# Moving the activation buffers 192 bytes on and leaving out three products per feed-forward stage

## The chip, the cores and the metric

The kernel runs on one NeuronCore of a Trainium2 chip. The metric is the device time of one execution in microseconds (us), lower is better. Before the change the median of three runs is 1860.11 us, the lowest 1859.53 and the highest 1865.53.

## What is computed

Ten layers in a row act on one sequence of 256 tokens with 1024 features (T = 256, D = 1024). Each layer normalises x, scales and shifts it by a modulation vector made from a condition c, applies a mixer or a feed-forward network, and adds the gated result to x:

```python
for st, kind in enumerate(["ffn", "mamba", "ffn", "ffn", "moba", "ffn", "sb", "cffn", "dsa", "cffn"]):
    shift, scale, gate = split(silu(c) @ mod_w[st] + mod_b[st], 3)
    h = rmsnorm(x, g[st]) * (1 + scale) + shift
    y = layer[kind](h)          # ffn: (silu(h @ w_gate) * (h @ w_up)) @ w_down, D_FF = 2816
    x = x + gate * y            # times 0.5 behind an ffn of the first block
```

"mamba" is a chunked state-space scan, "moba", "sb" and "dsa" are attention layers, "cffn" is a feed-forward network with a short convolution. All weights are float32 and each is used once: 276 blocks of 1 MB.

## The kernel before, in words

Everything is kept transposed: a tile has 128 partitions of features and 256 columns of tokens. A block of weights is a tile of 128 x 2048 float32. SyncE's queue loads block after block into six slots `raw0` to `raw5`. ScalarE rounds a block to a high part `w_hi` (type float32r, a form of float32 that TensorE multiplies in one pass), VectorE subtracts it from the block and writes the low part `w_lo`; there are three slots of each. The activations are split in the same way, into `h_hi` and `h_lo` behind the normalisation, and into `a_hi` and `a_lo` behind the nonlinearity. A product is then three matmuls by the helper `three`: high with high (L1413), high weights with the low activations (L1414), low weights with the high activations (L1415). Each is 128 x 128 stationary against 128 x 256 moving, and each has a weight load of its own (PEld in the profile) that overlaps the matmul before it. The stationary operand is the weights and the moving one the activations, with one exception: in "moba" and "sb" the value blocks (`tokens=True`) load `h` as the stationary operand and stream `w`.

A feed-forward stage has eleven triples of blocks (gate, up, down), 48 matmuls a block, in a fixed program order on TensorE: gate of block column n, up of n, down of n - 1. Semaphores order the engines: `wlo` counts finished splits, `blk` counts blocks that TensorE has finished with. The first gate block of a stage goes by a form of its own (L1426, L1428 and L1433): all products that need `h_hi` first, one feature tile after another as the normalisation delivers them, then those that need `h_lo`. Behind it the helper `in_step` issues three matmuls (L1453) in which the high part of the next block is both the stationary and the moving operand, into PSUM bank 6, where nobody reads them. The six feed-forward stages (four "ffn", two "cffn") share this program.

The buffers lie in SBUF in the order in which they are made. The program allots them one after another from a fixed start, each rounded up to a multiple of 32 bytes in every partition. These lines (L212 to L228) set what the change touches:

```python
raw = [sb(f"raw{s}", [P, 2048]) for s in range(NRAW)]
w_hi = [sb(f"w_hi{s}", [P, 2048], F32R) for s in range(NW)]
w_lo = [sb(f"w_lo{s}", [P, 2048], F32R) for s in range(NW)]
x = sb("x", [P, KT, T])
folded3 = sb("folded3", [P, 3, 96])
gs = sb("gs", [P, NJOB, 8])
h_hi = sb("h_hi", [P, KT, T], F32R)
```

Behind them follow `h_lo`, `work`, the modulation buffers, parameters and constants, `ws_hi` and `ws_lo` (a few small projection weights, also used through `three`), `a_hi`, `a_lo` and the large scratch tile `mix`. From the sizes in these lines: the six weight slots all start at the same remainder of 256 bytes (8192 bytes each); `h_hi` starts 6 x 8192 + 8192 + 1152 + 320 = 58816 bytes behind `w_hi0`, which is 229 x 256 + 192. `a_hi` starts 147904 bytes behind `w_hi0`, which is 577 x 256 + 192. So h and a both lie 192 bytes behind the weights by remainder of 256, which is the same as 64 bytes before them. Every slice that a matmul takes of w, h or a is a multiple of 512 bytes on, so this distance is the same in all of them. In the value blocks, where the operands change places, the moving one lies 64 bytes behind the stationary one.

Of the kernel before, what the change touches and what calls it, by code (L numbers as in the profile page):

```python
# [27 lines left out]
P = 128  # L28
T = 256
D = 1024  # L30
KT = D // P
# [179 lines left out]
def build(nc, weights, mods, params, consts, xin, out, stages=None):  # L211
# [3 lines left out]
    with ExitStack() as ctx:  # L215
        def sb(name, shape, dt=F32):
            return ctx.enter_context(nc.sbuf_tensor(name, shape, dt))
# [5 lines left out]
        folded3 = sb("folded3", [P, 3, 96])  # L223
        folded = [folded3[:, n, :] for n in range(3)]
        gs = sb("gs", [P, NJOB, 8])
        h_hi = sb("h_hi", [P, KT, T], F32R)
        h_lo = sb("h_lo", [P, KT, T], F32R)
        work = sb("work", [P, KT * T])  # L228
# [25 lines left out]
        bank = [ctx.enter_context(nc.psum_tensor(f"bank{n}", [P, 512], F32)) for n in range(8)]  # L254
# [1147 lines left out]
        def _(eng):  # L1402
            k = Steps(eng, plan, sems)

            def begin(st, i, a, b):

                eng.wait_ge(sems["wlo"], k.block(st, i, a, b) + 1)
                s = k.block(st, 0 if a % NW == 0 else i, a, b) % NW
                return [w[s][:, :] for w in (w_hi, w_lo)]
# [35 lines left out]
                                           kk == 0, kk == KT - 1)  # L1445
                mm.then_inc(sems["blk"], 1)

            def in_step(st, b):


                hi = begin(st, 0, 0, b)[0].rearrange("p (k n) -> p k n", k=KT)
                for kk in range(3):
                    eng.matmul(bank[6][:, 0:T], hi[:, kk, 0:P], hi[:, kk, :], start=True, stop=True)  # L1453

            def gemm_out(st, i=0, a=0, b=0, ready=None, fresh=False):

                hi, lo = [w.rearrange("p (k n) -> p k n", k=2) for w in begin(st, i, a, b)]
                for kk in range(2):
                    ready(kk)
                    for m in range(KT):  # L1460
                        part = slice(m * P, (m + 1) * P)
                        mm = three(acc(m), hi[:, kk, part], lo[:, kk, part], a_hi[:, kk, :], a_lo[:, kk, :],
                                   fresh and kk == m % 2 == 0, False, True)
                mm.then_inc(sems["blk"], 1)
# [32 lines left out]
            def ffn(st):  # L1497
                kind = stages[st]
                free4, per4, free5, per5 = ("silu", 1, "mul", 1) if kind == "ffn" else ("tap2", 2, "tap2", 2)

                def gate(i, a, b, first=False):
                    if not first:
                        k.wait(free4, st, i, per4, -per4)
                    gemm(bank[4], st, i, a, b, first=first)

                def up(i, a, b, first=False):
                    if not first:
                        k.wait(free5, st, i, per5, -1)
                    gemm(bank[5], st, i, a, b)

                def down(i, a, b, fresh=False):
                    gemm_out(st, i, a, b, lambda kk: k.wait("alo", st, i, 1, -1) if kk == 0 else None, fresh)

                gate(0, 0, 0, True)
                in_step(st, 1)
                up(0, 0, 1, True)
                gate(1, 3, -1)
                up(1, 3, 0)
                down(1, 3, 1, True)
                for i in k.loop(2, NFB - 1):  # L1520
                    gate(i, 3, -1)
                    up(i, 3, 0)
                    down(i, 3, 1)
                n = NFB - 1
                gate(n, 3, -1)
                up(n, 3, 0)
                down(n, 3, 1)
                last(st, lambda: k.wait("alo", st, b=n))

            def last(st, ready):  # L1530

                hi, lo = [w.rearrange("p (k n) -> p k n", k=2) for w in begin(st, 0, 0, NBLK[stages[st]] - 1)]
                ready()
                ffn = stages[st] in ("ffn", "cffn")
                ahi, alo = (z_hi, z_lo) if ffn else (a_hi, a_lo)
                more = st + 1 < NST
                if st == 0:
                    eng.wait_ge(sems["const"], 1)
                    eng.wait_ge(sems["late"], 2)
                    eng.wait_ge(sems["go"], KT + 2)  # L1540
                    eng.matmul(bank[7][:, 96:128], con_("fold"), gfold, start=True,
                               stop=True).then_inc(sems["gmods"], 1)
                if more:
                    modulation(st + 1)
                for pair in range(4):
                    if pair == 3 and more:
                        squares(st + 1, 0)
                    for m in (2 * pair, 2 * pair + 1):
                        part = slice(m * P, (m + 1) * P)
                        for kk in range(2):  # L1550
                            mm = three(acc(m), hi[:, kk, part], lo[:, kk, part], ahi[:, kk, :], alo[:, kk, :],
                                       False, False, True)
                    if pair < 3:
                        k.inc("pair", mm)
                    else:
                        mm.then_inc(sems["blk"], 1)
                if more:
                    squares(st + 1, 1)
                    squares(st + 1, 2)
                    squares(st + 1, 3)  # L1560
# [261 lines left out]
            def sparse_front(st):  # L1822
# [28 lines left out]
                for h in range(8):  # L1851
                    if h >= 2:
# [4 lines left out]
                k.wait("rel", st, b=7)  # L1857

            programs = {"ffn": ffn, "cffn": ffn, "mamba": mamba, "moba": lambda st: heads(st, "moba"),
                        "sb": lambda st: heads(st, "sb"), "dsa": lambda st: heads(st, "dsa")}  # L1860
            eng.wait_ge(s_ones, 16)
# [115 lines left out]
```

## Time and profile before

| | before |
|---|---|
| median of 3 runs | 1860.11 us (1859.53 to 1865.53) |
| the profiled execution | 1870.03 us, its span 1868.2 us |
| TensorE busy in the span | 1773.6 us, 95% |
| VectorE, ScalarE busy | 77%, 51% |
| mean granted clock of TensorE | 0.98 |
| DMA, mean over the span | 228 GB/s |

Busy shares alone tell little here. A matmul is pipelined, its recorded duration (about 280 ns) is longer than the distance to the next one, and TensorE is "busy" in 95% of the span whether its matmuls follow each other quickly or slowly. What tells is the distance between the starts of two matmuls, or, for a stretch without waits, the length of the stretch over the number of matmuls in it.

### The profile page before, as it was taken

To read this page: it belongs to the slowest core of one execution; us is meant where nothing else is said; L and a number is where in the kernel's file an instruction comes from. 1 tells how busy PE (TensorE), PEld (TensorE's weight loads), DVE (VectorE), ACT (ScalarE), POOL (GpSimd) and SP (SyncE) were. 2 spreads that over 40 slices of the span, in tenths; PEclk is the share of its full clock that TensorE was granted. 3 is DMA by queue.
4 is the path that set the end of the run, shared out by engine and by line. 5 is a ranking of instruction groups with operands and counts; after the bars stand their busy time and mean duration, and the time that the engine had idled before them with its cause. 6 is when DMAs were issued, how large, how long until landed. Compare 5 with 4: busy or idle time off the path is not lost.

```text
span 1868.2 us, 34057 instructions
## 1 busy us (share of the span) xinstructions
PE 1773.6 (95%) x14608; PEld 1718.4 (92%) x14608; DVE 1441.2 (77%) x1714; ACT 961.6 (51%) x1257; POOL 0.2 (0%) x4
## 2 busy tenths in 40 slices
PE   5999999999999999999989999898998999999999
PEld 4999999998899999999979999898898988889999
DVE  7799888887789779986557897655799777447776
ACT  4433466666434454445564433655644555666554
POOL 0000000000000000000000000000000000000000
PEclk8999999998999999999999999999999998999999
DMA  9999734433699759983426997243395534324551
GB/s 396 418 403 364 289 113 158 158 139 133 228 373 365 293 202 379 362 330 123 181 94 240 378 367 273 112 158 113 123 344 186 202 139 171 132 97 163 191 191 46
DMA packets 68149, 426.23 MB, mean 228 GB/s; under 512 B 7488, under 2 KB 10832, under 8 KB 31824
## 3 DMA queue, kind: packets, MB, share of 16 engines
q1 hardware_dynamic: 63936, 416.22, 58.3%
q10 hardware_dynamic: 4112, 8.62, 1.4%
q8 instruction: 68, 1.11, 0.2%
q14 instruction: 33, 0.27, 0.0%
HBM read 423.74 MB, written 3.17 MB: 229 GB/s over the span
## 4 chain that ended last, share of the span: by engine, by line
PE 85%; DVE 10%; ACT 3%; issue 2%; DMA 1%; DVEq 0%; SPq 0%; ACTq 0%
PE bank L1413 24%; PE bank L1414 24%; PE bank L1415 24%; DVE w_lo L839 3%; PE bank L1486 2%; DVE macc L880 2%; PE bank L1426 1%; PE bank L1428 1%; PE bank L1754 1%; PE bank L1433 1%; DMA mix<-mods 1%; DVE mix L1041 1%; PE bank L1596 1%; PE bank L1735 1%; DVE mix L857 1%
## 5 line engine op out<-in xcount | busy, mean ns | idle before, releaser
L1413 PE MATMUL bank<-h_hi,w_hi 128*128 128x256 f32 x2864 | 804.6, 281 | 13.2 <-DVE w_lo L839 12.7
L1414 PE MATMUL bank<-h_lo,w_hi 128*128 128x256 f32 x2864 | 798.3, 279 | 0.0
L1415 PE MATMUL bank<-h_hi,w_lo 128*128 128x256 f32 x2864 | 798.2, 279 | 0.0
L839 DVE TENSOR_TENSOR w_lo<-raw,w_hi 128x2048 fp32r<-128x2048 f32 x276 | 630.8, 2286 | 130.7 <-ACT w_hi L440 130.3
L440 ACT ACTIVATE w_hi<-raw 128x2048 fp32r<-128x2048 f32 x276 | 527.7, 1912 | 151.5 <-PE bank L1415 139.9
L1413 PEld LDWEIGHTS bank<-h_hi,w_hi 128*128 128x128 f32 x2864 | 541.4, 189 | 18.4 <-DVE w_lo L839 14.4
L1415 PEld LDWEIGHTS bank<-h_hi,w_lo 128*128 128x128 f32 x2864 | 542.6, 189 | 0.0
L1414 PEld LDWEIGHTS bank<-h_lo,w_hi 128*128 128x128 f32 x2864 | 540.3, 189 | 0.1
L1413 PE MATMUL bank<-a_hi,w_hi 128*128 128x256 f32 x1280 | 359.0, 280 | 0.0
L1414 PE MATMUL bank<-a_lo,w_hi 128*128 128x256 f32 x1280 | 356.1, 278 | 0.0
L1415 PE MATMUL bank<-a_hi,w_lo 128*128 128x256 f32 x1280 | 356.1, 278 | 0.0
L1413 PEld LDWEIGHTS bank<-a_hi,w_hi 128*128 128x128 f32 x1280 | 241.3, 188 | 1.8 <-issue 1.0
L1415 PEld LDWEIGHTS bank<-a_hi,w_lo 128*128 128x128 f32 x1280 | 242.2, 189 | 0.0
L1414 PEld LDWEIGHTS bank<-a_lo,w_hi 128*128 128x128 f32 x1280 | 241.0, 188 | 0.1
L880 DVE SCALAR_TENSOR_TENSOR macc<-modws,cact,macc 128x1536 f32<-128x1536 f32 x126 | 226.0, 1811 | 1.2 <-DMA modws<-mods 1.1
L1041 DVE SCALAR_TENSOR_TENSOR mix<-bank,par,mix 128x254 f32<-128x254 f32 (+1 forms) x176 | 76.7, 477 | 47.5 <-ACT mix L519 46.0
L493 ACT ACTIVATE a_hi<-mix 128x512 fp32r<-128x512 f32 x40 | 25.2, 631 | 147.5 <-PE bank L1415 118.7
L479 ACT ACTIVATE mix<-bank 128x512 f32<-128x512 f32 x44 | 26.3, 599 | 124.9 <-PE bank L1415 121.5
L519 ACT ACTIVATE mix<-bank,par 128x256 f32<-128x256 f32 x88 | 44.8, 560 | 81.0 <-PE bank L1415 77.8
L1426 PE MATMUL bank<-h_hi,w_hi 128*128 128x256 f32 x160 | 49.9, 338 | 23.7 <-ACT h_hi L468 23.7
L1426 PEld LDWEIGHTS bank<-h_hi,w_hi 128*128 128x128 f32 x160 | 39.1, 244 | 27.1 <-issue 27.1
L1486 PE MATMUL bank<-work,con 128*128 128x256 f32 x160 | 42.2, 403 | 20.9 <-ACT work L456 20.9
(261 smaller groups left out, 1663.5 us busy)
## 6 DMA issues: line engine op xcount, KB each, us to landing
raw<-weights SPq DMA_DIRECT2D x276, 1024.0 KB, 5.0
modws<-mods SPq DMA_DIRECT2D x144, 768.0 KB, 6.7
mix<-mods SPq DMA_DIRECT2D x5, 1024.0 KB, 8.8
mix<-mods ACTq DMA_DIRECT2D x8, 512.0 KB, 13.9
biases<-scratch ACTq DMA_DIRECT2D x1, 2048.0 KB, 14.7
mix<-biases ACTq DMA_DIRECT2D x4, 512.0 KB, 3.8
modws<-mods SPq DMA_DIRECT2D x1, 1024.0 KB, 11.8
x<-xin SPq DMA_DIRECT2D x1, 1024.0 KB, 11.0
```

Of the source, the lines that this page charges most:

```text
L440: eng.activation(w_hi[g % NW][:, :], raw[g % NRAW][:, :], ACT.Copy).then_inc(sems["whi"], 1)
L479: k.inc("silu", eng.activation(sg, bank[4][:, :].rearrange("p (a t) -> p a t", a=2), ACT.Silu))
L493: k.inc("ahi", eng.activation(z_hi if final else a_hi[:, :, :], act, ACT.Copy))
L519: ins = eng.activation(dst[:, m, :], b[:, m * T:(m + 1) * T], ACT.Identity, scale=cw(i, t, 2), bias=cw(i, t, 3))
L839: eng.tensor_tensor(w_lo[g % NW][:, :], raw[g % NRAW][:, :], w_hi[g % NW][:, :], ALU.subtract).then_inc(sems["wlo"], 1)
L880: ins = eng.scalar_tensor_tensor(out=m, in0=modw[q % 4], scalar=c, in1=m, op0=ALU.mult, op1=ALU.add)
L1041: ins = eng.scalar_tensor_tensor(out=dst[:, m, lag:T], in0=b[:, m * T:(m + 1) * T - lag], scalar=cw(i, 22 * up + m, tap), in1=dst[:, m, la ...
L1413: eng.matmul(dst, ah, bh, start=start, stop=False, skip_group_check=skip)
L1414: eng.matmul(dst, ah, bl, start=False, stop=False, skip_group_check=skip)
L1415: return eng.matmul(dst, al, bh, start=False, stop=stop, skip_group_check=skip)
L1426: eng.matmul(d, hi[:, kk, part], h_hi[:, kk, :], start=kk == m == 0, stop=False, skip_group_check=True)
L1486: mm = eng.matmul(bank[6][:, r * T:(r + 1) * T], con_("ones"), (sq2 if r else work3)[:, m, :], start=m == r == 0, stop=m == KT - 1, skip_g ...
```

## The change

One unused buffer of 192 bytes a partition is put between `gs` and `h_hi`, so that all buffers from `h_hi` on start 192 bytes later, and `in_step` with its call is taken out. The distance from the weights to h and a becomes 59008 = 230 x 256 + 128 bytes for `h_hi`, and likewise for `a_hi`: 128 by remainder of 256, in either direction. Buffers behind the gap keep their distances from each other, buffers before it theirs.

```diff
         gs = sb("gs", [P, NJOB, 8])
+        gap = sb("gap", [P, 48])
         h_hi = sb("h_hi", [P, KT, T], F32R)
...
-            def in_step(st, b):
-
-
-                hi = begin(st, 0, 0, b)[0].rearrange("p (k n) -> p k n", k=KT)
-                for kk in range(3):
-                    eng.matmul(bank[6][:, 0:T], hi[:, kk, 0:P], hi[:, kk, :], start=True, stop=True)
-
...
                 gate(0, 0, 0, True)
-                in_step(st, 1)
                 up(0, 0, 1, True)
```

## Rows read from the trace of the kernel before

**Rows 1.** The page: busy time and share by engine, and the chain by engine.
```profile
PE 1773.6 (95%) x14608; PEld 1718.4 (92%) x14608; DVE 1441.2 (77%) x1714; ACT 961.6 (51%) x1257; POOL 0.2 (0%) x4
PE 85%; DVE 10%; ACT 3%; issue 2%; DMA 1%; DVEq 0%; SPq 0%; ACTq 0%
```
**Rows 2.** Groups of TensorE by form: count, busy us, mean ns, idle us before.
```profile
L1413 PE MATMUL bank<-h_hi,w_hi 128*128 128x256 f32 x2864 | 804.6, 281 | 13.2 <-DVE w_lo L839 12.7 <-ACT mix L806 0.6
L1413 PE MATMUL bank<-a_hi,w_hi 128*128 128x256 f32 x1280 | 359.0, 280 | 0.0
L1413 PE MATMUL bank<-w_hi,h_hi 128*128 128x256 f32 x128 | 36.5, 285 | 1.4 <-ACT mix L694 1.4
```
**Rows 3.** Windows, TensorE: stretch, us, busy (matmuls), granted clock, DMA share, GB/s.
```profile
43.00:134.00 91.00, 91.00 (x805) 1.00 1.02 418
155.50:221.20 65.70, 65.70 (x560) 1.00 0.92 360
480.60:655.80 175.20, 175.20 (x1489) 1.00 0.85 330
675.30:761.80 86.50, 86.50 (x765) 1.00 0.88 335
...
992.10:1167.10 175.00, 175.00 (x1488) 1.00 0.85 330
...
1691.10:1859.10 168.00, 168.00 (x1485) 1.00 0.43 156
```
**Rows 4.** Windows over two whole "ffn" stages: us, then busy (count) per engine.
```profile
480.60:660.20 179.60, 179.60 (x1528) 179.60 (x1528) 154.07 (x106) 74.42 (x58) 0.00 (x0) 1.00 0.85 327
675.20:848.00 172.80, 172.80 (x1526) 172.80 (x1526) 152.04 (x105) 74.30 (x58) 0.00 (x0) 1.00 0.88 340
```
**Rows 5.** Timeline, third and last matmul of three 48-matmul blocks of mixers.
```profile
868.84 0.28 PE L1415 MATMUL bank<-w_hi,h_lo 128*128 128x256 f32 x1
874.14 0.28 PE L1415 MATMUL bank<-w_hi,h_lo 128*128 128x256 f32 x1
...
883.08 0.28 PE L1415 MATMUL bank<-h_hi,w_lo 128*128 128x256 f32 x1
888.18 0.28 PE L1415 MATMUL bank<-h_hi,w_lo 128*128 128x256 f32 x1
...
1285.64 0.28 PE L1415 MATMUL bank<-w_hi,h_lo 128*128 128x256 f32 x1
1290.94 0.28 PE L1415 MATMUL bank<-w_hi,h_lo 128*128 128x256 f32 x1
```
**Rows 6.** Timeline around the three extra products, two stages: start, us, instructions.
```profile
674.21 0.50 PE L1433 MATMUL bank<-h_lo,w_hi 128*128 128x256 f32 x3
674.55 0.51 PE L1453 MATMUL bank<-w_hi 128*128 128x256 f32 x3
674.89 0.28 PE L1413 MATMUL bank<-h_hi,w_hi 128*128 128x256 f32 x1
...
479.85 0.64 PE L1433 MATMUL bank<-h_lo,w_hi 128*128 128x256 f32 x4
480.32 0.52 PE L1453 MATMUL bank<-w_hi 128*128 128x256 f32 x3
480.67 0.28 PE L1413 MATMUL bank<-h_hi,w_hi 128*128 128x256 f32 x1
```
**Rows 7.** Timeline of the small projection of "mamba", stationary 32 columns of ws.
```profile
239.76 0.28 PE L1413 MATMUL bank<-h_hi,ws_hi 128*32 128x256 f32 x1
239.99 0.28 PE L1415 MATMUL bank<-h_hi,ws_lo 128*32 128x256 f32 x1
240.34 0.28 PE L1415 MATMUL bank<-h_hi,ws_lo 128*32 128x256 f32 x1
240.70 0.28 PE L1415 MATMUL bank<-h_hi,ws_lo 128*32 128x256 f32 x1
241.75 0.28 PE L1415 MATMUL bank<-h_hi,ws_lo 128*32 128x256 f32 x1
242.09 0.28 PE L1415 MATMUL bank<-h_hi,ws_lo 128*32 128x256 f32 x1
```
**Rows 8.** Waits of TensorE: us in total, times, longest.
```profile
PE bank L1426 <- ACT h_hi L468: 23.7, 10, 4.5
PE bank L1413 <- DVE w_lo L839: 12.7, 8, 4.1
```

## The prediction

> **What bounds the kernel now.** I read the page first. TensorE is busy 95% of the span and makes up 85% of the chain that ended last [rows 1]. The groups say with what: the products of the helper `three`, 128 x 128 against 128 x 256; L1413 alone has 2864 of them with h, 1280 with a and 128 with the operands exchanged, L1414 and L1415 as many each, 12,816 in all, of which 384 are exchanged [rows 2]. The waits of TensorE are small beside that: 23.7 us for `h_hi` at the ten stage starts, 12.7 us for `w_lo` [rows 8]. So the question is how closely the matmuls follow each other.
>
> The windows over stretches without a wait answer it, and the reader is to divide two columns: the stretch by the number of matmuls. Three stretches give 168.0 / 1485, 86.5 / 765 and 91.0 / 805, that is 113.1, 113.1 and 113.0 ns a matmul. Three others, of the same program and mostly of the same "ffn" code, give 175.2 / 1489, 175.0 / 1488 and 65.7 / 560, that is 117.7, 117.6 and 117.3 ns [rows 3]. The granted clock is 1.00 in all of them (the 2.4 GHz level), TensorE never sits idle, and the DMA load doesn't sort them: 113.0 ns stands at 418 GB/s, 117.7 ns at 330. There are **two paces, 4.5 ns apart**, and a stage keeps the one it begins with. The two whole "ffn" stages show the price: 179.60 us for 1528 matmuls and 172.80 for 1526, 6.8 us for the same work [rows 4]. The blocks of the mixers show the same two, from the third to the 48th matmul, 45 distances: 868.84 to 874.14 and 1285.64 to 1290.94 in blocks with exchanged operands, 5.30 us or 117.8 ns each; 883.08 to 888.18 in an ordinary block, 5.10 us or 113.3 ns [rows 5].
>
> The exchanged blocks have the slow pace in eight of eight; [rows 5] show the first and the last. There the moving operand lies 64 bytes behind the stationary one by remainder of 256, everywhere else 64 bytes before it. That is the trace's one sign that the distance counts.
>
> **The three products taken out.** From the first L1453 to the next L1413 it is 674.55 to 674.89 and 480.32 to 480.67, 0.34 and 0.35 us [rows 6]. Six stages have them: 6 x 0.35 = **2.1 us**, all on the path, since the next block's `w_lo` is there (no wait stands before the L1413 behind them). In the first stage 418 GB/s of loads set the pace for some time [rows 3], so 0.35 us of it may come back as a wait: 1.7 to 2.1 us. What they do besides is open. They may be meant to set the pace, but in the trace they hand it on: before them three L1433 take 0.34 us (113 ns), and behind them the fast pace goes on; in the other stage four take 0.47 us (118 ns), and behind them the slow pace goes on [rows 6]. All six stages behave so. I put their effect on the pace at nothing. The cover for that is that the pace is kept, and if it is gone, a stage may change either way, by 6.8 us each [rows 4]: two stages could win it, four could lose it.
>
> **The 192 bytes.** No instruction is added and none takes another shape; VectorE's `w_lo` split works wholly on buffers before the gap, and products whose operands are both behind the gap keep their distance. What changes is the distance of the 12,432 ordinary products, from 64 bytes before to 128, and of the 384 exchanged ones, from 64 behind to 128. The trace of before holds no product of full size at 128, so this needs bounds. The nearest rows are those of the small projection, with only 32 stationary columns: its weights step by 160 bytes from one feature tile to the next, so its eight tiles run through eight distances. At the first tile the moving operand is 128 from the stationary one, and two matmuls take 239.76 to 239.99, 0.23 us, 115 ns each. At the third it lies 64 behind: 240.34 to 240.70, three in 0.36 us, 120 ns. At the seventh it lies 64 before: 241.75 to 242.09, 0.34 us, 113 ns [rows 7]. So 64 before is the best there, 64 behind the worst, and 128 between them, nearer to the best. That fits the exchanged blocks. It bounds the new pace: from 113.1, the fast one, to some 118 or 120 ns.
>
> Which value in between? The two paces are steady states, and they are discrete: the row at 115 ns is of too few matmuls to be a third one. I take the fast pace as the only one left at 128, by two reasons from the rows. The slow pace is what the worst distance, 64 behind, always gives; 128 is 64 bytes away from it on either side and no less for the exchanged products, whose own distance becomes as good as the others'. And what sits at 128 in the small projection is not in the range of the worst.
>
> Then the slow stretches become fast. Three of them are in [rows 3], 1489 + 1488 + 560 = 3537 matmuls x (117.6 - 113.1) = 15.9 us. The remaining slow ones are 29 stretches of 33 to 94 matmuls inside mixers and the first "cffn", 1464 matmuls (the two slow blocks of [rows 5] stand for them): x 4.5 = 6.6 us. Together **22.5 us**. VectorE and ScalarE have room: they are busy for 154 and 74 us of a slow stage of 179.6, and the stage that runs at the fast pace has the same work on them in 172.80 us without a wait [rows 4]. The loads: a stage at 330 GB/s would ask for 343, and one runs at 352 to 418. Only the slow stretch at 360 GB/s, in the first stage, might turn part of its 2.5 us into waits for `w_lo`.
>
> **The sum**, against the profiled execution of 1870.0 us (span 1868.2, with 1.8 around it): 1870.0 - 22.5 - 2.1 = **1845.4, say 1846 us**. The median of before, 1860.1, lies 9.9 us under the profiled execution and the highest of the three 4.5 under it. That fits the paces: one "ffn" stage at the other pace is worth 6.8 us, so the runs differ in what stages they run slowly. If no stretch is slow any more, the result doesn't depend on that, and the runs should also agree better. The gain against the median is 14 us, 0.8%.
>
> The Trainium skill speaks against this gain. "TensorE: Matmul & The Clock Gate", section "Step-by-step: what each phase is for", says that TensorE has two independent read ports, and that loading the next tile's weights takes no bandwidth from the running matmul; by this no distance between the operands could matter. Its section "Back-to-back issue gap" gives N / 2.4 + 2.5 ns, 109.2 ns for 256 columns by an estimate from that page; no window of full-size products shows that, the best is 113.0.
>
> **Rivals.**
>
> *The slow pace rules (slower).* At 128 the reads of the next weights and of the moving operand meet where they can't slip past each other, and every product has the pace that the exchanged ones have now. For it: the small projection at 128 took 115 ns and not 113, and exchanging operands at 64 was enough to lose the fast pace altogether. Against it: it is nearer to the best than to the worst. Price: of some 12,816 + 480 products of this shape (the first blocks' 480 included) 5001 are slow, 8300 would become so: 8300 x 4.5 = 37 us, less 2.1, gives 1870.0 + 37 - 2.1 = 1905; about 3 us of it would hide in the first stage, where the loads set the pace at 418 GB/s [rows 3], so 1902. It decides from the point where more than half of the 8300 lose the fast pace. If only the stages' long stretches do, 1870 to 1890.
>
> *The distance doesn't matter (as the skill's rule would have it) or only mixes otherwise.* Both paces stay, drawn at each stage start as before, and the exchanged blocks are slow for another reason. For it: the same distance now gives both paces, so distance alone doesn't set them. Against it: exchanged blocks, eight of eight. Then only the 2.1 us go: 1860.1 - 2.1 = 1858, with a spread of a stage or so, 1850 to 1866.
>
> *A new, faster pace.* If the 4 ns over the estimate above came from reads that meet, and 128 ended that too, 12,800 x 3.9 ns = 50 us more would go, 1796. Against it: the record shows no full-size stretch under 113.0, at any load, and the small projection, with a quarter of the stationary columns, is not faster either (0.34 us for three at its best) [rows 7].
>
> **Chances and range.** The forecast 48%, the slow pace 28%, both as before 18%, a new pace 6%. By its own terms the forecast goes from 1838 (some loss at the starts also goes) to 1852 (some blocks stay slow). The range holds that, the case of both paces, and most of the slower case: 1838 to 1902. A measurement of this kernel tells about 0.3% from no change, 5.6 us: faster is under 1854.5, slower over 1865.7. Faster: 0.48 + 0.06 and a fifth of the mixed case, 0.57; same: the most of the mixed case, 0.14; slower: 0.28 and what the mixed case leaves, 0.29.
>
> **What would show it.** Right: all six feed-forward stages at 113.1 ns by windows over them, none at 117.6; mean duration of L1413 at 276 to 277 ns; exchanged blocks at the others' pace; no L1453, and L1413 right behind L1433. The small projection keeps its distances (both operands are behind the gap), so its 0.36 us for three stays: a control. Wrong: any long stretch at 117.6 ns or above (the distance doesn't set the pace, or sets it the other way); stages that start fast and turn slow behind the first block would say that the three products held the pace; more waits for `w_lo` than 12.7 us would say that the loads took the gain back.

## The result, and the profile after

| | before | after |
|---|---|---|
| median | 1860.19 us (1859.53 to 1865.53) | 1907.03 us (1903.38 to 1912.44) |
| profiled execution | 1870.03 us, span 1868.2 | 1908.27 us, span 1906.5 |
| TensorE busy | 1773.6 us | 1818.1 us |

The change makes the kernel slower: the ratio is 1.0248, with a 95% interval from 1.0216 to 1.0279. The forecast was 1846 us; the rival "the slow pace rules", with 1902 us, came nearest.

The lines of the products are one further down in the changed file: L1414, L1415 and L1416 are what L1413, L1414 and L1415 were. These windows of the changed kernel answer [rows 3]; the columns are stretch, length in us, busy us and number of matmuls, granted clock, DMA share and GB/s:

```profile
41.90:138.40 96.50, 96.50 (x815) 1.00 0.98 409
...
491.40:667.80 176.40, 176.40 (x1489) 1.00 0.85 328
685.50:861.80 176.30, 176.30 (x1488) 1.00 0.85 328
1014.40:1190.70 176.30, 176.30 (x1488) 1.00 0.85 328
1720.80:1902.80 182.00, 182.00 (x1536) 1.00 0.40 147
```

Each is 118.4 to 118.5 ns a matmul by division of its columns. By the starts of the first and last matmul, which the edges of a window don't touch, it is 118.66 or 118.67 ns in every long stretch; six short ones, some 300 products, run at 120.0. There is **one pace in the long stretches where there were two**, and it is slower than both: the same starts give 113.3 and 117.8 ns in the windows of [rows 3]. The load doesn't matter (147 or 409 GB/s), nor does the stage. Over all stretches of more than 30 such matmuls without a wait the mean went from 115.2 to 118.7 ns, of some 12,700 distances in either trace.

Groups of TensorE by form, for [rows 2], and its waits, for [rows 8]:

```profile
L1414 PE MATMUL bank<-h_hi,w_hi 128*128 128x256 f32 x2864 | 814.3, 284 | 9.9 <-DVE w_lo L840 9.2 <-ACT mix L807 0.8
L1414 PE MATMUL bank<-a_hi,w_hi 128*128 128x256 f32 x1280 | 365.1, 285 | 0.0
```

```profile
PE bank L1427 <- ACT h_hi L469: 23.7, 10, 4.5
PE bank L1480 <- ACT work L457: 20.2, 3, 19.2
PE bank L1414 <- DVE w_lo L840: 9.2, 6, 3.6
```

The same count of products, each some 3 to 5 ns longer, and 3.5 us less waiting for `w_lo`, as one would expect where TensorE asks for it later. With that the time adds up: some 13,000 products at full clock x (118.7 - 115.2) = 45.5 us more, less 2.1 for the products taken out, less 3.5 of the waits, makes 39.9; the profiled executions differ by 38.2.

Against [rows 5], the first block with exchanged operands, third to 48th matmul: 5.34 us in 45 distances, 118.7 ns. It has the others' pace, as the forecast had it, but the wrong one.

```profile
887.85 0.28 PE L1416 MATMUL bank<-w_hi,h_lo 128*128 128x256 f32 x1
...
893.19 0.28 PE L1416 MATMUL bank<-w_hi,h_lo 128*128 128x256 f32 x1
```

### The profile page after: what moved, and what is told of

It is laid out like the page before. It is cut to its first block, busy times and chain, and to the rows that moved or that the text cites. A ratio compares the mean times of both kernels' runs of the same rounds, so it can differ in the third digit from the quotient of the medians.

```text
span 1906.5 us, 34021 instructions
## 1 busy us (share of the span) xinstructions
PE 1818.1 (95%) x14590; PEld 1762.6 (92%) x14590; DVE 1442.5 (76%) x1714; ACT 961.6 (50%) x1257; POOL 0.2 (0%) x4
## 4 chain that ended last, share of the span: by engine, by line
PE 87%; DVE 8%; ACT 3%; issue 1%; DMA 1%; DVEq 0%; SPq 0%; ACTq 0%
PE bank L1414 25%; PE bank L1416 25%; PE bank L1415 24%; DVE w_lo L840 3%; PE bank L1480 2%; PE bank L1427 1%; DVE macc L881 1%; PE bank L1429 1%; PE bank L1747 1%; PE bank L1434 1%; DMA mix<-mods 1%; DVE mix L1042 1%; PE bank L1589 1%; PE bank L1728 1%; PE bank L1624 0%
## 5 line engine op out<-in xcount | busy, mean ns | idle before, releaser
L1414 PE MATMUL bank<-h_hi,w_hi 128*128 128x256 f32 x2864 | 814.3, 284 | 9.9 <-DVE w_lo L840 9.2
L1416 PE MATMUL bank<-h_hi,w_lo 128*128 128x256 f32 x2864 | 808.3, 282 | 0.0
L1415 PE MATMUL bank<-h_lo,w_hi 128*128 128x256 f32 x2864 | 808.2, 282 | 0.0
L1414 PEld LDWEIGHTS bank<-h_hi,w_hi 128*128 128x128 f32 x2864 | 541.9, 189 | 14.4 <-DVE w_lo L840 10.6
L1415 PEld LDWEIGHTS bank<-h_lo,w_hi 128*128 128x128 f32 x2864 | 542.0, 189 | 0.1
L1416 PEld LDWEIGHTS bank<-h_hi,w_lo 128*128 128x128 f32 x2864 | 541.6, 189 | 0.0
L1414 PE MATMUL bank<-a_hi,w_hi 128*128 128x256 f32 x1280 | 365.1, 285 | 0.0
L1415 PE MATMUL bank<-a_lo,w_hi 128*128 128x256 f32 x1280 | 362.2, 283 | 0.0
L1416 PE MATMUL bank<-a_hi,w_lo 128*128 128x256 f32 x1280 | 362.1, 283 | 0.0
L1414 PEld LDWEIGHTS bank<-a_hi,w_hi 128*128 128x128 f32 x1280 | 243.3, 190 | 1.8 <-issue 1.0
L1415 PEld LDWEIGHTS bank<-a_lo,w_hi 128*128 128x128 f32 x1280 | 243.2, 190 | 0.1
L1416 PEld LDWEIGHTS bank<-a_hi,w_lo 128*128 128x128 f32 x1280 | 243.1, 190 | 0.0
L1006 DVE TENSOR_TENSOR a_lo<-mix,a_hi 128x512 fp32r<-128x512 f32 x40 | 27.6, 690 | 46.1 <-ACT a_hi L494 46.1
```

Source lines behind the costliest of these rows:

```text
L1006: k.inc("alo", eng.tensor_tensor(z_lo if final else a_lo[:, :, :], act, z_hi if final else a_hi[:, :, :], ALU.subtract))
L1414: eng.matmul(dst, ah, bh, start=start, stop=False, skip_group_check=skip)
L1415: eng.matmul(dst, ah, bl, start=False, stop=False, skip_group_check=skip)
L1416: return eng.matmul(dst, al, bh, start=False, stop=stop, skip_group_check=skip)
```

## The experiments

**The two halves of the change, and addresses without distances.** The theory was by then that the distance between the stationary and the moving operand, by remainder of 256 bytes, sets the pace (theory A in what was expected). The rivals: the three products had held stages at the fast pace, so that their removal is the cause (B); the remainder of an address itself counts (C); or other engines' accesses do (D).

The gap alone, the three products kept:

```diff
         gs = sb("gs", [P, NJOB, 8])
+        gap = sb("gap", [P, 48])
```

> The kernel before with the 192 bytes alone, the three extra products of each feed-forward stage kept. Theory A (the distance between the operands sets the pace): as the changed kernel and 2 us above it, about 1909 us, every stretch at 118.4 to 118.8 ns a matmul. Theory B (the three products held the stages at the fast pace, the distance does nothing): 1860 to 1870 us, with long stretches at 113 ns.

Measured: 1910.49 us (1905.84 to 1913.71), ratio 1.025 (1.0181 to 1.032). The gap alone makes the loss. Windows:

```profile
492.30:670.70 178.40, 178.40 (x1489) 1.00 0.85 324
690.30:866.60 176.30, 176.30 (x1488) 1.00 0.86 328
```

One of its stages runs at 120.0 ns by its starts and the others at 118.7, so this distance too has more than one steady pace.

The products alone taken out:

```diff
                 gate(0, 0, 0, True)
-                in_step(st, 1)
                 up(0, 0, 1, True)
```

> The kernel before without the three extra products of each feed-forward stage, no buffer moved. Theory A (they only hand the pace on): 1858 us, within 6 us by which stages run slowly, both paces 113.1 and 117.6 ns still there. Theory B (they hold the fast pace): the changed kernel's time, about 1900 us, no long stretch at 113 ns.

Measured: 1869.33 us (1859.30 to 1879.16), ratio 1.0025 (0.9991 to 1.0058). In its trace both paces stand, as before:

```profile
671.00:846.00 175.00, 175.00 (x1489) 1.00 0.85 330
994.60:1163.10 168.50, 168.50 (x1488) 1.00 0.87 343
```

So the fast pace doesn't need the three products: without them stages still run at either. Their own 2.1 us can't be seen under a spread of 20 us between runs. But they seem to act on the pace, which the trace of before alone didn't show. In this run, without them, all six feed-forward stages go on behind their first block at the pace that they had in it; only two of them came slow. With them, and with the distance of before, the traces of before and of the two runs with all addresses moved and with a gap of 256 bytes (both below) hold seven stage starts that came to them at 117.8 ns without a wait: four went on at 113.3 ns. All ten that came at 113.3 ns stayed there. Here is one of the four, from the run with all addresses moved: seven products ahead take 0.82 us, 117 ns each, and the window behind is the second one shown for that run, at 113.2 ns:

```profile
480.20 0.99 PE L1434 MATMUL bank<-h_lo,w_hi 128*128 128x256 f32 x7
481.02 0.53 PE L1454 MATMUL bank<-w_hi 128*128 128x256 f32 x3
```

A stage that turns is worth 6.8 us [rows 4], so they may well be worth more than they cost. The times don't settle it: the interval of the ratio goes from 1.7 us faster to 10.8 us slower without them. At the distance of the change they can't have held the fast pace: with the gap and with them no stage reached it, and the one at 120.0 ns left 118.5 ns at these very products.

All addresses moved, no distance:

```diff
+        gap = sb("gap", [P, 48])
         raw = [sb(f"raw{s}", [P, 2048]) for s in range(NRAW)]
```

> The kernel before with the 192 bytes ahead of all buffers instead of between weights and activations: every address moves, no distance does. Theory A (only the distance between stationary and moving operand counts): as before, 1860 us within 6, both paces. Theory C (the remainder of an address itself counts, for TensorE, for the loads or for another engine): slower, up to 1907 us.

Measured: 1865.69 us (1854.34 to 1868.62), ratio 0.9987 (0.9953 to 1.002). No difference; both paces are there, in this trace with the first stage slow up to its waits (95.9 us for 816) and the later ones fast:

```profile
41.20:137.10 95.90, 95.90 (x816) 1.00 0.99 415
481.40:649.90 168.50, 168.50 (x1489) 1.00 0.86 343
```

So this shift of all remainders does nothing, which speaks against theory C.

**TensorE by itself.** A small program loads one tile, copies it to four buffers at the same remainder, and issues the kernel's triples with the moving slice a number of bytes further on. No other engine works while it runs.

```diff
+            for off in range(0, 64, 8):                 # 0, 32, ... 224 bytes
+                for start in range(3):
+                    ...                                 # one, two or three short products
+                    gemm(off)                           # 48 products each
+                    gemm(off)
```

> TensorE alone on the chip's core, no other engine working, with the same triples of 128 x 128 against 128 x 256: the moving operand 0, 32, 64, ... 224 bytes behind the stationary one by remainder of 256, each distance three times, behind one, two or three short products, 96 matmuls each time, at last 48 products with 32 stationary columns at each distance. It leaves out the whole computation. Theory A: at 192 both 113.1 and 117.6 ns or the first alone, at 64 117.8 ns, at 128 118.4 to 118.8 ns, other distances open. Theory D (other engines' reads and writes of the same memory make the difference): one pace at all distances. If a distance gives under 113 ns or gives 113.1 whatever stands before, it is the one to try in the kernel.

Windows over 96 matmuls, 95 distances, at 0, 32, 64, 64 (behind three short products), 96, 128, 160, 192 and 224 bytes (the counts in brackets take in the end of what stands before):

```profile
21.07:32.55 11.48, 11.48 (x99) 1.00 0.01 1
56.28:67.46 11.18, 11.18 (x99) 1.00 0.00 0
90.57:101.42 10.85, 10.85 (x98) 1.00 0.01 2
112.92:124.16 11.24, 11.24 (x97) 1.00 0.01 1
124.31:135.78 11.47, 11.47 (x98) 1.00 0.00 1
159.52:170.88 11.36, 11.36 (x99) 1.00 0.01 1
194.37:205.61 11.24, 11.24 (x99) 1.00 0.00 0
228.97:239.84 10.87, 10.87 (x99) 1.00 0.01 2
262.32:273.64 11.32, 11.32 (x98) 1.00 0.01 1
```

The first and the third differ by 0.63 us in 11 for the same instructions at another distance, at a granted clock of 1.00, with VectorE, ScalarE and the DMA engines idle. Left without its first half, each stretch settles at a pace of its own: at 0 bytes 120.0 ns, at 32 116.7, at 64 113.3 or 117.8 by what stands before, at 96 120.0, at 128 118.6 to 118.7, at 160 117.4 or 118.6, at 192 113.3, at 224 118.3. The values of the whole kernel are among them: 113.3 and 117.8 of before, 118.7 of after. So TensorE makes the paces by itself, and theory D, other engines, is out.

The last part of the same program repeats the small projection's shape, 32 stationary columns, and here the ground falls on which the prediction ranked the distances. At 0, 64, 128 and 192 bytes, 48 products, 47 distances:

```profile
297.07:302.41 5.34, 5.34 (x50) 1.00 0.00 0
308.22:313.71 5.49, 5.49 (x50) 1.00 0.02 3
319.52:324.96 5.44, 5.44 (x51) 1.00 0.01 3
330.58:336.23 5.65, 5.65 (x51) 1.00 0.00 0
```

That is 113.6, 116.8, 115.7 and 120.2 ns, and 113.3, 116.7, 115.5 and 120.0 over the last 24. With 128 columns 192 is the best of these and 0 the worst, with 32 columns it is the other way round. The 115 ns that [rows 7] have at 128 were right for its shape, and told nothing of this one.

**Do these values hold for the kernel?** Two gaps in the whole kernel, 64 bytes (distance 0) and 256 bytes (distance 192 again), the three products kept:

```diff
-        gap = sb("gap", [P, 48])
+        gap = sb("gap", [P, 16])     # and [P, 64]
```

> The kernel before with a gap of 64 bytes: h and a at the remainder of the weights, distance 0. Theory A (distance sets the pace, by the values that TensorE alone showed): 120 ns everywhere, so some 13,000 products x (120.0 - 115.2, the mean of before) = 62 us more than the profiled execution of before, 1925 to 1932 us, slower than the changed kernel. A smooth dependence with 128 as the point farthest from the best one at 192 or 64 (conflict by nearness alone) would give about the changed kernel's time, 1907 us.

Measured: 1924.42 us (1919.20 to 1926.94), ratio 1.0335 (1.0298 to 1.0371), and 120.0 ns by the starts in all long stretches:

```profile
493.20:671.60 178.40, 178.40 (x1489) 1.00 0.85 324
689.70:868.10 178.40, 178.40 (x1489) 1.00 0.85 324
```

The profiled execution took 1926.94 us where the map gave 1925 to 1932.

> The kernel before with a gap of 256 bytes: the distance by remainder of 256 stays 192, every buffer behind it moves. Theory A: as before, 1851 to 1876 us, both paces. If the period of the pattern is longer than 256 bytes, another pace: 116 to 120 ns and 1880 us or more.

Measured: 1865.85 us (1859.44 to 1874.79), ratio 1.0023 (0.9992 to 1.0055), the same as before, with both paces:

```profile
42.50:138.40 95.90, 95.90 (x817) 1.00 0.99 409
483.00:651.40 168.40, 168.40 (x1488) 1.00 0.87 343
```

Between these two placements, 256 bytes apart, nothing changes; other periods were not tried.

**A finer map.** The same small program in steps of 16 bytes with six beginnings (two short products of 40, 72, ... 200 columns), from 160 to 224 in steps of 4 with the same six, and once over all 64 distances with three of them:

```diff
-            for off in range(0, 64, 8):
+            for off in range(0, 64, 4):      # 16 bytes; range(40, 57) and range(0, 64): 4 bytes
```

> TensorE alone again, computation left out: distances 0, 16, 32, ... 240 bytes, each with six beginnings, 48 products each. If the pace is a smooth function of the distance, the steps between will give values between those of the steps of 32 (120.0 at 0, 116.7 at 32, 113.3 or 117.8 at 64, 120.0 at 96, 118.6 at 128, 117.4 to 118.7 at 160, 113.3 at 192, 118.3 at 224). If what counts is a unit of 32 bytes or more, pairs of neighbours will be alike. At 192 and 64 some of the six beginnings should end at 117.8 ns, as stages of the whole kernel do at 192.

> TensorE alone, computation left out: distances 160 to 224 bytes in steps of 4, six beginnings each. If there is a distance near 192 at which all beginnings end at 113.3 ns, it is the one to try in the kernel, and worth some 10 us there; if 192 is the only one under 117 ns, nothing is to be had by the distance alone.

> TensorE alone, computation left out: all 64 distances in steps of 4 bytes, three beginnings each. Distances 0, 96 and 112 should give 120.0, 120.0 and 113.3 ns again; 64 and 192 113.3 or 117.8. If the pace followed a single zone of nearness, there would be one broad minimum; by the steps so far there are several narrow ones. A value under 113.3 ns would be new.

Mean of the last 24 distances of each product in ns, by the starts in the traces of the four small programs; where beginnings differ, both ends:

```
bytes      0      16        32        48     64        80         96     112
ns       120.0 116.7-118.7 116.6-117.8 118.3 113.3-117.8 118.3-120.0 120.0 113.3
bytes    128      144       160       176    192       208        224    240
ns    118.5-118.8 113.3-118.6 117.3-120.0 119.2-119.4 113.3-117.8 116.7-119.2 118.3 117.0-117.3
```

The steps of 4 bytes in between lie at 116.8 to 124.4 ns. There is no broad minimum. Good distances are single points: 188 gives 118.6 to 118.9 and 196 gives 121.4 to 121.7 beside the 113.3 or 117.8 of 192. Nothing is faster than 113.3, and **112 is the one distance where all beginnings ended there**, six of six and three of these once more; 108 gives 120.0 and 116 gives 121.8. Where paces differ, the short products alone don't decide: at 192 the same six gave 117.8 every time behind the products at 176 bytes, and 113.3 in four of six behind those at 188. The last 24 distances at 108, 112 and 116 bytes, with the first beginning (2.88, 2.72 and 2.92 us between their first and last start; the window of 112 takes in a little more):

```profile
505.96:508.84 2.88, 2.88 (x26) 1.00 0.00 0
523.77:526.50 2.73, 2.73 (x27) 1.00 0.00 0
541.02:543.95 2.93, 2.93 (x27) 1.00 0.03 6
```

**The kernel at 112 bytes.** Without the three products; h and a each in one tile, from its fifth element on, behind gaps of 160 and 224 bytes:

```diff
-        h_hi = sb("h_hi", [P, KT, T], F32R)
-        h_lo = sb("h_lo", [P, KT, T], F32R)
+        gap = sb("gap", [P, 40])
+        h = sb("h", [P, 2 * KT * T + 8], F32R)
+        h_hi, h_lo = (h[:, 4 + KT * T * n:4 + KT * T * (n + 1)].rearrange("p (k t) -> p k t", k=KT) for n in range(2))
...                                     # the same for a_hi and a_lo, behind gap_a of 224 bytes
```

> The kernel before without the three extra products, and h and a 112 bytes behind the weights by remainder of 256, where TensorE alone took 113.3 ns from all of six beginnings (the 384 exchanged products then lie at 144, 116.7 to 118.7 ns). Theory A (the map of TensorE alone holds for the kernel): nearly all ordinary products at 113.3 ns, 1846 to 1850 us, 0.8% under the kernel before, and runs that lie closer together than its 1851 to 1876. Theory E (the beginnings in the kernel reach other steady states than the six tried): a mixture, 1855 to 1875 us or more.

Measured: 1849.42 us, ratio to before 0.9922 (0.9893 to 0.9951), 0.8% faster than the kernel before and 3% than the changed one. The time is the one expected. Its seven runs lie within 1847.95 to 1852.85, where twelve of the kernel before, on the same chip, spread from 1856.24 to 1875.62. Windows over its long stretches:

```profile
42.10:134.40 92.30, 92.30 (x817) 1.00 1.01 424
478.30:646.80 168.50, 168.50 (x1488) 1.00 0.88 343
664.20:832.80 168.60, 168.60 (x1490) 1.00 0.88 342
981.30:1149.80 168.50, 168.50 (x1489) 1.00 0.87 343
1673.40:1841.90 168.50, 168.50 (x1489) 1.00 0.43 156
```

All at the fast pace, 113.3 to 113.4 ns by the starts. One part was expected wrongly: the exchanged blocks, now at 144 bytes, take 120.0 ns and not 116.7 to 118.7; here the third and last matmul of the first, 5.40 us in 45 distances:

```profile
858.26 0.28 PE L1417 MATMUL bank<-w_hi,h 128*128 128x256 f32 x1
...
863.66 0.28 PE L1417 MATMUL bank<-w_hi,h 128*128 128x256 f32 x1
```

The small program never exchanged operands. Its map of 144 bytes has several steady states, so this may be one more, or the map of exchanged operands may be another; no run tells. At the other distances that the kernels tried, the exchanged blocks have values of their distance: 120.0 ns at 0, 117.8 at 64, 118.7 at 128 (120.0 in two blocks of the run with the gap alone).

## Why the prediction was wrong

**What bounds the kernel** was read rightly: the pace of the products. Two paces 4.5 ns apart, at any load: that held, and TensorE alone shows the same two. That a stage keeps the pace it begins with holds for stretches without a wait and behind the first block. The first stage of before runs at 113.3 ns, waits for `w_lo` twice (5.6 us in all) and goes on at 117.8 [rows 3]; with all addresses moved it is the other way round. The reading of the spread between runs fits too. A longer series of the kernel before ranges from 1850.9 to 1876.1 us, which is several stages of 6.8 us at one pace or the other, and the kernel at 112 bytes, with the fast pace alone, has a quarter of the spread.

**The three products.** Their own 2.1 us agree with the sum above, and no run shows them alone. Their effect on the pace was put at nothing, because all six stages of one trace handed it on. At the distance of before that looks wrong: in other traces stages turned from slow to fast right at them, four of seven with those of before. It did not decide the result: at the new distance the run that keeps them is as slow as the one without.

**The 192 bytes** is the step that failed: the ordinary products at 128 bytes were put at the fast pace, 113.1 ns, and they take 118.7. The bounds themselves, 113.1 to 118 or 120 ns, held it; wrong was the place between them, for two reasons. First the ranking. I took the nearest rows for 128 bytes from the small projection, whose shape is 32 stationary columns, and from two or three matmuls per distance. Neither carried over. In the steady state the 32-column shape is best at 0 and worst at 192, the 128-column shape nearly the reverse. And two or three matmuls are a passage, not a pace: I read 0.36 us for the three of the third tile as "the worst distance" and named it a control that the change would not touch. After the change, with that distance the same, they take 0.35 us (246.46 to 246.81; 349 ns by the starts in the trace, where before had 357). With all addresses moved and no distance changed they take 350 ns, so three matmuls differ by what stands before them:

```profile
246.46 0.28 PE L1416 MATMUL bank<-h_hi,ws_lo 128*32 128x256 f32 x1
...
246.81 0.28 PE L1416 MATMUL bank<-h_hi,ws_lo 128*32 128x256 f32 x1
```

The eight exchanged blocks were a sign of the slow pace at 64 bytes, but not of a zone around it. TensorE alone takes 117.8 ns there with ten of twelve beginnings and 113.3 with two. And 64 bytes further on, at 128, the pace is slower still.

Second the rule for going from one distance to another: "128 is 64 bytes away from it on either side". This supposes that the pace changes smoothly with the distance. The map says otherwise: 96 gives 120.0, 112 gives 113.3, 128 gives 118.7. I also took it that the two paces seen were the only ones, "a third one" dismissed by the few matmuls. The third was the answer.

**The sum** fails with that: where it had 22.5 us less for the slow stretches, the runs show 45 us more for all of them.

**The rival "the slow pace rules"** had the right sign and nearly the time, by the wrong price: it took the pace of 117.6 ns for all (37 us); the pace is 118.7. That it came within 5 us is in part luck. Its reason, that reads "can't slip past each other" at 128, is not shown by any run. The rival by which the distance doesn't matter is refuted by the gap of 64 bytes, +3.35% for the same instructions. It rested on what the Trainium skill says in "TensorE: Matmul & The Clock Gate", section "Step-by-step: what each phase is for", of two independent read ports. The measured paces don't agree with what was drawn from it: whatever the ports are, the distance between the streamed and the stationary operand costs up to 11 ns in 113 (124.4 ns at 132 bytes). What the skill states in "SBUF — State Buffer", section "Who interferes with whom", that TensorE waits on no other engine, agrees with the runs: 113.3, 117.8, 118.7 and 120.0 ns stand in the kernels and with all other engines idle. The new pace below 113 ns, the fourth rival, is found at none of the 64 distances.

What is not settled is the mechanism inside. That it is the read of the next weights that meets the read of the moving operand is argued from the dependence on their distance alone; no run took the weight load away. Nor does any run say why the same distance has several steady paces.

## What to carry to other kernels

Where a tuned kernel's matmuls follow each other without waits, divide a window by its count; a few ns over the best stretch of the same shape, kept through whole stages, can be a steady state of TensorE that depends on where the two operands lie to each other, as it was here. It can be mapped in one small program for the shape at hand, and a distance where every beginning ends at the fast pace is worth more than one that is fast sometimes: it takes the spread out as well. Don't interpolate such a map, and don't bound one shape by another or a pace by three instructions.

## What was not expected of the hardware

The paces are sharp and repeat over stages and runs: 113.33, 117.78, 118.67 and 120.0 ns for 128 x 128 against 128 x 256 in float32r at the granted clock of 1.00 (the 2.4 GHz level). One step of 4 bytes can change the pace by 8.5 ns (112 to 116 bytes: 113.3 to 121.8). At one and the same distance what stands before decides between paces, and in the traces a pace once reached lasts for 1488 matmuls. At three products with the same tile as both operands 117.8 ns turned into 113.3 for the rest of a stage in four of seven cases, and the reverse in none of ten; two slow stages without such products stayed slow.
